# A chunkwise recurrence on one core: decay applied to the queries, and 64-row halves for the products beside it

## The reference

```
m_t = max(b + m, max_s(log_D));  inter_w = exp(b + m - m_t)
s   = (q k^T) * exp(log_D - m_t)
num = s v + inter_w * (q C);     den = sum(s) + inter_w * (q n)
h   = num / max(|den|, exp(-m_t))
C   = decay * C + (ws * k)^T v;  n likewise
```

## Time and profile before

| | |
|---|---|
| median of 3 runs | 1169.8 us (1169.3 to 1170.23) |
| the profiled execution, first to last instruction (span) | 1168.5 us |
| median of the runs less that span | 1.3 us |
| TensorE busy | 1158.7 us, 99% |
| weight loads (PEld) busy | 946.1 us, 81% |
| VectorE, GpSimd, ScalarE busy | 678.5, 455.9, 359.2 us |
| granted TensorE clock, mean | 0.999 of full speed |
| front of head 0 (calls and scores) | 486.6 to 498.9 us |
| recurrence, heads 0 to 3 | 498.9 to 677.2 us |

### The profile page before, as it was taken

How to read it: one execution, slowest core, us unless ns; L and a number is a source line. 1 busy time by engine, 2 the same in 40 slices (tenths; PEclk the granted TensorE clock), 3 DMA queues, 4 the chain that set the end, 5 groups by cost and what they waited for, 6 DMA issues and landing times.

```text
span 1168.5 us, 17252 instructions
## 1 busy us (share of the span) xinstructions
PE 1158.7 (99%) x6599; PEld 946.1 (81%) x6599; DVE 678.5 (58%) x1249; ACT 359.2 (31%) x720; POOL 455.9 (39%) x437
## 2 busy tenths in 40 slices
PE   9999999999999999999999999999999999999997
PEld 6888888888888868888878888878988887777786
DVE  5645557334368502157777883894699434556668
ACT  6312121100012212445665631242111134553322
POOL 2424222223333223354657656304223323455534
PEclk9999999999999999999999999999999999999999
DMA  7321121343312112300113242123121130133113
GB/s 241 109 81 45 36 81 36 123 152 114 109 36 72 64 64 90 101 23 23 50 34 112 88 171 73 72 100 95 40 88 36 37 100 1 38 122 124 39 38 141
DMA packets 75075, 93.56 MB, mean 80 GB/s; under 512 B 13938, under 2 KB 54090, under 8 KB 74483
## 3 DMA queue, kind: packets, MB, share of 16 engines
q1 hardware_dynamic: 67270, 88.73, 22.7%
q10 hardware_dynamic: 7724, 3.74, 1.2%
HBM read 75.11 MB, written 18.92 MB: 80 GB/s over the span
## 4 chain that ended last, share of the span: by engine, by line
PE 93%; DVE 4%; DMA 1%; ACT 1%; issue 1%; POOL 0%; ACTq 0%; DVEq 0%; POOLq 0%
PE bank L918 22%; PE bank L920 22%; PE bank L919 22%; PE bank L1219 4%; PE bank L1194 4%; PE wide L1210 2%; PE wide L1412 2%; PE bank L1158 1%; PE bank L1147 1%; PE bank L1135 1%; PE wide L920 1%; PE wide L919 1%; PE wide L918 1%; PE bank L1387 1%; DVE h L1910 1%; PE wide L1387 1%
## 5 line engine op out<-in xcount | busy, mean ns | idle before, releaser
L687 POOL CAST whi<-wraw 128x2048 fp32r<-128x2048 f32 x31 | 58.8, 1898 | 454.1 <-PE bank L920 404.1
L918 PE MATMUL bank<-u_hi,wlo 128*128 128x512 f32 x488 | 190.4, 390 | 0.0
L920 PE MATMUL bank<-u_hi,whi 128*128 128x512 f32 x488 | 189.9, 389 | 0.0
L919 PE MATMUL bank<-u_lo,whi 128*128 128x512 f32 x488 | 189.9, 389 | 0.0
L689 POOL TENSOR_TENSOR wlo<-wraw,whi 128x2048 fp32r<-128x2048 f32 x32 | 153.1, 4784 | 3.0 <-ACT whi L2488 0.5
L918 PE MATMUL bank<-x_hi,wlo 128*128 128x512 f32 x312 | 123.5, 396 | 0.0
L920 PE MATMUL bank<-x_hi,whi 128*128 128x512 f32 x312 | 121.6, 390 | 0.0
L919 PE MATMUL bank<-x_lo,whi 128*128 128x512 f32 x312 | 121.5, 389 | 0.0
L918 PEld LDWEIGHTS bank<-u_hi,wlo 128*128 128x128 f32 x488 | 91.6, 188 | 19.9 <-POOL wlo L689 0.8
L920 PEld LDWEIGHTS bank<-u_hi,whi 128*128 128x128 f32 x488 | 91.6, 188 | 19.0
L919 PEld LDWEIGHTS bank<-u_lo,whi 128*128 128x128 f32 x488 | 91.6, 188 | 18.9
(11 more groups left out here) (391 smaller groups left out, 2440.9 us busy)
## 6 DMA issues: line engine op xcount, KB each, us to landing
wraw<-in_w_in SPq DMA_DIRECT2D x26, 1024.0 KB, 5.5
wraw<-in_w_out SPq DMA_DIRECT2D x12, 1024.0 KB, 5.1
xr<-in_x SPq DMA_DIRECT2D x8, 512.0 KB, 7.3
hst<-in_x SPq DMA_DIRECT2D x4, 1024.0 KB, 5.0
hpool<-hst SPq DMA_DIRECT2D x4, 1024.0 KB, 4.1
smz<-mzs SPq DMA_DIRECT2D x16, 256.0 KB, 2.0
h<-hpool SPq DMA_DIRECT2D x4, 1024.0 KB, 7.5
resid<-h SPq DMA_DIRECT2D x8, 512.0 KB, 2.6
```

The costliest lines, as they stand in the source:

```text
L687: g_.tensor_copy(whi[w % 2][:, :, :], wraw[:, :, :]).then_inc(s["w_hi"], 1)
L918: pe.matmul(ps, al, bh, start=(k == 0), stop=False)
L919: pe.matmul(ps, ah, bl, start=False, stop=False)
L920: return pe.matmul(ps, ah, bh, start=False, stop=(k == nk - 1))
```

## The change

The decay of the positions moves from the inter product's result to the queries, and the inter product then adds up in the same bank as Pm times v. The rows of decay (`r4[:, 0, :]`) are stored beside the stabilisers in DRAM and spread with them, so a spread moves 256 KB instead of 128. GpSimd multiplies the queries of unit n+2 by the spread row (`scale_q`) in its turn for unit n, into four buffers `qsi`, `qsj`. ScalarE's scaled copy and VectorE's `total` go.

The calls of `headwise` for keys and values become half as many and twice as long: eight blocks, each in two halves of 64 rows, the halves into two neighbouring banks. Queries in units 0 to 3, keys in 4 and 6, values in 8 and 10; none in 5, 7, 9 and 11. `turn_h` of heads 0 to 2 is made of halves too, in banks 0 and 1. The queries' calls and scores alternate between banks 0 and 1. ScalarE empties a keys' call with one instruction of 1024 elements, a values' call with two of 512.

```diff
-    nm_t = nc.dram_tensor("nmax", [ROWS, P], F32)
+    nm_t = nc.dram_tensor("nmax", [ROWS, 2, P], F32)
...
-        FILL = {m: (m,) for m in range(12)}
+        FILL = {0: 0, 1: 1, 2: 2, 3: 3, 4: 4, 6: 5, 8: 6, 10: 7}
...
 # SyncE
-                    sp_.dma_start(nm_t.ap(), nM[:, :]).then_inc(s["o_rel"], 16)
-                    sp_.wait_ge(s["o_rel"], 32)
+                    sp_.dma_start(nm_t.ap()[:, 0, :], nM[:, :]).then_inc(s["o_rel"], 16)
+                    sp_.wait_ge(s["a_r"], 3)
+                    sp_.dma_start(nm_t.ap()[:, 1, :], r4[:, 0, :]).then_inc(s["o_rel"], 16)
+                    sp_.wait_ge(s["o_rel"], 48)
...
 # GpSimd
+            def scale_q(n):
+                h, p, d, ck, _ = unit(n)
+                i = upd_of(h, p - 1, d)
+                if d == 0:
+                    g_.wait_ge(s[f"l_br{n // 2 % 4}"], 16 * (n // 8 + 1))
+                if i >= 4:
+                    g_.wait_ge(s["t_inter"], i - 3)
+                g_.tensor_tensor(scaled_q(i), qTs[h % 2][:, :, ck * P:(ck + 1) * P],
+                                 carried(n // 2, d).unsqueeze(1).to_broadcast([P, 2, P]), ALU.mult
+                                 ).then_inc(s["g_qs"], 1)
...
                     if n % 2 == 0 and n < 62:
                         masked(n // 2 + 1)
+                    if n % 16 < 14:
+                        scale_q(n + 2)
                     if n in GATE_MUL:
                         gate_mul(GATE_MUL[n])
...
 # TensorE
-            turns, free = [0], [1, 5, 2, 6, 3, 7]
+            turns, free = [0], [5, 6, 7, 4]
...
+                both(m2, "a_hq", 10 * h + (i + 1 if i < 6 else 2 * i - 4))
+                if i == 6:
+                    pe.wait_ge(s["g_bdh"], 2 * h + 2)
+                for block in range(8):
+                    t, m = i % 2 * 4 + block // 2, block % 2
+                    tt = slice(t * P, (t + 1) * P)
+                    for half in range(2):
+                        rows = slice(64 * half, 64 * half + 64)
+                        out_ = bank[2 * m2 + half][:, block * 64:(block + 1) * 64]
+                        if i < 6:
+                            mm = pe.transpose(out_, cc[rows, 2 * h + m, tt],
+                                              cst[rows, C_ID + 64 * half:C_ID + 64 * half + 64])
                         else:
-                            mm = pe.matmul(ps[:, b * P:(b + 1) * P], um[:, 2 * h + m, tt], bdh[:, m, :],
-                                           start=True, stop=True)
+                            mm = pe.matmul(out_, um[rows, 2 * h + m, tt], bdh[rows, m, rows], start=True, stop=True)
...
+                    sums = take(4 + n % 4, "v_h", n + 1)
                     if p:
                         i = upd_of(h, p - 1, d)
+                        pe.wait_ge(s["g_qs"], i + 1)
                         pe.wait_ge(s["v_C"], 2 * i + 2)
-                        ps = take(0, "a_tmp", i + 1)
                         for k in range(2):
-                            mm = pe.matmul(ps[:, 0:AUG], q[:, k, ck * P:(ck + 1) * P], Cst[:, d, k, :],
-                                           start=(k == 0), stop=(k == 1))
+                            mm = pe.matmul(sums[:, 0:AUG], scaled_q(i)[:, k, :], Cst[:, d, k, :],
+                                           start=(k == 0), stop=False)
...
                     pe.wait_ge(s["g_P"], n + 1)
-                    ps = take(4 + n % 4, "v_h", n + 1)
-                    pe.matmul(ps[:, 0:AUG], Pm[:, n % 2, :], v[:, ck, :], start=True, stop=True
+                    pe.matmul(sums[:, 0:AUG], Pm[:, n % 2, :], v[:, ck, :], start=(p == 0), stop=True
                               ).then_inc(s["t_intra"], 1)
...
 # VectorE
-                    total(h, n)
                     if p or h in (0, NH - 1):
                         state(h, n)
-                    total(h, n + 1)
-                    if p:
-                        ve.wait_ge(s["v_tot"], upd_of(h, p - 1, 1) + 1)
+                    ve.wait_ge(s["t_intra"], n + 2)
...
 # ScalarE
-                    if p:
-                        i = upd_of(h, p - 1, d)
-                        ps = filled(ac, "t_inter", i + 1, "a_tmp", i + 1)
-                        if n >= 4:
-                            ac.wait_ge(s["v_h"], n - 3)
-                        ac.activation(tmps[p % 2][:, d, :], ps[:, 0:AUG], ACT.Copy, scale=cols[:, 0, r:r + 1]
-                                      ).then_inc(s["a_tmp"], 1)
```

More of the change, by code:

```diff
@@ L238, in build @@
          cva, mzs, _m, wgx, gx, gr, ga, wkx, kx, ak,
-         hc0, yt0, kwb, Amat, hc1, Cst, tmpi, Pm, bdh, gs, nM, cols,
+         hc0, yt0, kwb, Amat, hc1, Cst, qsi, Pm, bdh, gs, nM, cols,
          rif, rl, rb, r4, rz, rp, rpc, rms8, rn,
@@ L307, in build @@
         rcx = sb("rcx", [P, 2, 2])
-        bank = [ctx.enter_context(nc.psum_tensor(f"bank{i}", [P, 512], F32)) for i in range(4)]
+        duo = [ctx.enter_context(nc.psum_tensor(f"bank{m}", [P, S], F32)) for m in range(2)]
         wide = [ctx.enter_context(nc.psum_tensor(f"wide{m}", [P, S], F32)) for m in range(2)]
-        bank += [wide[i // 2][:, i % 2 * 512:(i % 2 + 1) * 512] for i in range(4)]
+        duo += wide
+        bank = [duo[i // 2][:, i % 2 * 512:(i % 2 + 1) * 512] for i in range(8)]
         names = (
@@ L1124, in fill, with both, headwise @@
                 return take(free[turns[0] % len(free)], name, value)
-            def headwise(h, i):
-                n, i = i // 4, i % 4
-                if n == 0:
+            def both(m, name, value):
+                take(2 * m, name, value)
+                return take(2 * m + 1, name, value)
+            def headwise(h, i, m2=0):
+                if i < 4:
                     m, nh = i // 2, i % 2
@@ L1167, in turn_h @@
                 if h < NH - 1:
-                    ps = fill("a_t1", n + 1)
-                else:
-                    ps = ring_x("v_y1", 12 + 2 * i + 1)
+                    both(0, "a_t1", n + 1)
+                    for b in range(4):
+                        for half in range(2):
+                            rows = slice(64 * half, 64 * half + 64)
+                            mm = pe.transpose(bank[half][:, b * 64:(b + 1) * 64],
+                                              hcs[h % 2][rows, 4 * nh + b, mt * P:(mt + 1) * P],
+                                              cst[rows, C_ID + 64 * half:C_ID + 64 * half + 64])
+                    mm.then_inc(s["t_h"], 1)
+                    return
+                ps = ring_x("v_y1", 12 + 2 * i + 1)
                 for b in range(4):
@@ L1223, in units @@
                         turn_h(h - 1, TURN[n % 16])
-            for i in range(12):
-                headwise(0, i)
+            for i in range(8):
+                headwise(0, i, i % 4)
+            free[:] = [0, 1]
             for b in range(2):
                 scores(0, b)
-            del free[1:]
             for h in range(NH):
@@ L2341, in evac_features @@
                                   ).then_inc(s["a_hq"], 1)
[L2342 to L2345, removed]
+                    return
+                ac.wait_ge(s["t_hw"], 8 * h + i + 1)
+                t = slice(i % 2 * 4, i % 2 * 4 + 4)
+                if i < 6:
+                    ac.activation(kts[h % 2][:, t, :].rearrange("p t (m u c) -> p u (t m) c", m=2, c=64),
+                                  duo[m2][:, :].rearrange("p (u b c) -> p u b c", u=2, c=64), ACT.Copy
+                                  ).then_inc(s["a_hq"], 1)
+                    return
+                for half in range(2):
+                    ac.activation(vs[h % 2][:, t, 0:HD].rearrange("p t (m u c) -> p u t m c", m=2, c=64)[:, half],
+                                  bank[2 * m2 + half][:, :].rearrange("p (t m c) -> p t m c", t=4, c=64), ACT.Copy
+                                  ).then_inc(s["a_hq"], 1)
             def evac_scores(h, b):
@@ L2434, in units @@
                         turned_h(4 * (h - 1) + TURN[m])
-            for i in range(8):
-                evac_features(0, i)
+            for i in range(6):
+                evac_features(0, i, i % 4)
             ac.wait_ge(s["v_cols"], 1)
             weight(0)
-            for i in range(8, 12):
-                evac_features(0, i)
+            for i in range(6, 8):
+                evac_features(0, i, i % 4)
             for b in range(2):
```

88 lines of the change are left out of this document (41 added, 47 removed).

## The result

The change takes 1172.8 us (median of 5 runs, 1172.53 to 1175.31) against 1169.74 for the kernel before on the same chip: ratio 1.0031, 95% interval 1.0019 to 1.0042. The forecast was 1166.1 us and "faster"; both were wrong. The profiled execution's span is 1171.0 us against 1168.5.

The account below looks back on a forecast made before the run. The prediction took TensorE, busy 99% of the span, to bound the kernel. Its terms summed to −3.7 us, taking the profiled span from 1168.5 to 1164.8 and the median to 1166.1 us, range 1162.5 to 1172.

Parts of the forecast that it names:

- keys in halves, six calls: Six key calls beside the recurrence: sixteen half transposes cost 0.83 us against 0.87 for eight full ones, −0.2 us.
- turns in halves: Turns on TensorE's path in heads 1, 2 and first in 3: eight halves 0.58 us against 0.44, +1.3 us.
- values in halves, six calls: Six value calls beside the recurrence: 1.33 us each in halves against 1.79 full, −2.7 us (−3.3 to +2.0).
- front of head 0: Before head 0, two key and two value calls in a row share one switch: −1.9 us.
- stalls after the table loads: Third unit of heads 1 to 3: waits behind ScalarE's table loads, tmp and Cst come back in full, −1.7 us.
- turned bank: Behind turns: TensorE's waits for the bank ScalarE is still emptying come back, −1.8 us.
- units 33 and 49: Second unit of heads 2 and 3: scaling on GpSimd makes Pm late, +0.65 and +0.25, together +0.9 us.
- end of head 3: Last eight units, no filler left: five scalings on GpSimd delay Pm, +2.4 us, bounds 0 and 3.5.
- no overlap: Upper bound for a value call in halves, 16 × 64 × 1.76 ns + 0.33 = 2.13 us.
- rival 2: Value halves don't overlap, 2.13 us each instead of 1.33, also before head 0: +6.4, 1172.5 us; chance 0.1.
- rival 3: TensorE's stalls stay because another wait ends last in their place: +3.5, 1169.6 us, no difference; chance 0.2.
- rival 1: GpSimd becomes the bound in all heads, if a scaling costs about 0.98 us, not 0.73: 1174 us; chance 0.15.

Follow-up runs that it names:

- full products for the values: The changed kernel with the values' calls as eight full products of 128 rows in two banks, all else kept: 1170.8 us.
- unscaled queries: The changed kernel without any scaling of the queries, the decay left out of the inter product: 1168.33 us.
- keys on ScalarE: The changed kernel with head 3's weighted keys made by ScalarE instead of GpSimd, query scaling staying on GpSimd: 1169.75 us.
- narrow moving data: The changed kernel with 32 instead of 64 moving columns in each values' half product, weights unchanged: 1173.93 us in one run.

## Why the prediction was wrong, point by point

| term | predicted, us | measured, us | shown by |
|---|---|---|---|
| keys in halves, six calls | −0.2 | −0.2 | starts at 601.17 |
| turns in halves | +1.3 | +1.2 (8 of them; the others lie in head 3's end) | starts at 658.27 |
| values in halves, six calls | −2.7 | +2.0 | full products for the values |
| front of head 0 | −1.9 | −0.4 | starts at 486.23, 494.47 |
| stalls after the table loads | −1.7 | −1.75 | starts at 601 |
| turned bank | −1.8 | −1.55 | starts behind turns |
| units 33 and 49 | +0.9 | +1.15 | unscaled queries |
| end of head 3 | +2.4 | +2.6 | unscaled queries, keys on ScalarE |
| sum | −3.7 | +3.1 (the windows: +3.2) | |

The step that failed is "Values": "I take 32 records at 0.031 = 1.0", and the same rate for 96 records in front of head 0. These two terms are off by 4.7 and 1.5 us, 6.2 of the 6.9 us between the forecast's sum and that of the windows. The 0.031 came from transposes and was carried over to fp32 products. I had checked it against the score products of 64 rows and 32 output rows, which load only 32 weight columns and stream 288: a form in which the load can't be the bound, so it said nothing about this one. What is true of the earlier trace rows is that row halves overlap; here they overlap too (starts 1 ns apart), but a full product does the work of two halves in the same two passes. Sixteen pairs of half passes take 1.84 us (half of the 3.67 in front of head 0), as do sixteen full ones (half of 3.68 at the same place with full products), and the mode switch comes on top. The bound "no overlap", 2.13, was met to the digit by another mechanism.

So rival 2, chance 0.1, met the time by luck: 1172.5 forecast for it, 1172.8 measured. Its reason, that the halves don't overlap, is refuted by their starts and by narrow moving data: one behind the other, half the stream would have shortened the call. The Trainium skill (TensorE: Matmul & The Clock Gate, section LDWEIGHTS) has a load last its columns over 1.2 GHz, however few rows. For the values the trace agrees: 0.11 us for a pair of passes with 128 weight columns, 0.06 with 64 (there with half the output rows as well). The prediction set this rule aside because transposed halves take 0.062, which they still do, so the sentence "it doesn't bear that out" was true of transposes and was applied to the wrong kind of product. By the page's rule the call would have been 2.04 and the kernel about 1171.7 us; the measured call is 2.13.

The other steps held. The stalls named did go, with their sizes, once the decay was moved; rival 3 (another wait takes their place) is refuted by the kernel with only the decay moved, where none of them is left. Of the turned bank's waits, 2.0 us when all starts behind turns are compared, 0.11 stayed at each of four score calls (1.00 and 1.86 us where 0.97 and 1.78 are free), so 1.55 came back. GpSimd was priced rightly at the end of head 3 (+2.4, got +2.6) and a little low at units 33 (+0.7 with its neighbours) and 49 (+0.45, its update in unit 48 followed by 1.26 us instead of 0.86). In unit 33 the query call is followed by 1.49 us instead of 0.86, as Pm stands behind scaling and gating. The timeline there, all engines, kernel after:

```profile
590.99 1.26 POOL L787 TENSOR_TENSOR yt<-yt,smzb 128x512 f32<-128x512 f32 x1
591.23 1.02 PE L1166 MATMUL bank<-cc,Amat 128*128 128x512 f32 x2
...
592.21 0.46 POOL L808 TENSOR_TENSOR Pm<-ST,Wb 128x128 f32<-128x128 f32 x1
```

Pm starts 592.21 and had started 591.79 before, in a head that now begins 0.3 us earlier: the 0.70 us of one scaling.

One figure of the working is off without effect: the prediction's own costs add up to 44.9 us for TensorE in head 2, not "some 44.6", which moves rival 1's threshold for a scaling only a little.

The range of 1162.5 to 1172.0 missed the result by 0.8 us: its upper edge left rival 2 outside, though its working stood at 1172.5 with a bound of the values' row behind it.

## What to carry to other kernels

Before a rate is carried from one product to another, ask what sets it in the form where it was seen (stream, weight load, or a single pass against two), and take it only from a form with the same weight columns, the same passes and a stream as short. Splitting rows in halves pays where each half runs in less than a full pass, as the transposes do, and long rows of them share one switch (about 0.1 us on either side); a full fp32 product of 128 weight and 128 moving columns, split in two, gained nothing here. When work moves to an engine with room on average, price it in the stretch that has no filler left (here the last eight units), and move something else off that engine there in the same edit.

## What the runs showed of the hardware that was not expected

- Two row halves of an fp32 product with 128 weight columns and 64 moving columns take 0.11 us a pass together, as a full pass does (0.89 us for 8). With 32 moving columns nothing changes; with 64 weight columns it is 0.06. The transposed halves have the same form in the trace, 64 by 128 with 64 columns, and take 0.062 in a single pass, their loads 138 ns instead of 188. Why a transpose's load is the faster one no run here shows.
- VectorE and GpSimd slowed each other down where a VectorE operation with two operands in SBUF ran beside GpSimd. In the kernel after this is more frequent: VectorE's mix of the turned head (L1798) took 733 to 1552 ns, 994 in the mean of 11, against 785 in the mean of 12 before, and six of 64 Pm took 0.84 to 0.92 us, about twice the usual 0.45; before, none took over 0.47. Without any scaling (the unscaled kernel) the mix took 814 ns in the mean of 12, but six Pm were as long. So the scaling accounts for most of the longer mixes and not for the long Pm. The timeline of the kernel after:

```profile
571.33 1.28 POOL L795 TENSOR_TENSOR ym_lo<-yt,ym_hi 128x512 fp32r<-128x512 f32 x1
571.61 1.54 DVE L1798 SCALAR_TENSOR_TENSOR yt<-cc,VT,yt 128x512 f32<-128x512 f32 x1
...
572.55 0.91 POOL L808 TENSOR_TENSOR Pm<-ST,Wb 128x128 f32<-128x128 f32 x1
```

  VectorE ends only after GpSimd's 1.28 us, and the Pm that starts at 572.55 ends 0.3 us behind VectorE instead of after 0.46. The Trainium skill (SBUF — State Buffer, section SBUF: two separate sides) says that the two share a pair of ports that one instruction holds alone, also when a VectorE operation has two SBUF inputs; these rows and the 2.09 us pair of scalings on VectorE agree that each waits for the other. They don't show that the one that waits stands still: VectorE is done 0.54 us after GpSimd, less than the 0.73 of its shortest such operation. It is at least a part of why moving the scaling to VectorE, where it took 0.69 us in the mean (0.41 at the least) in place of 0.73, saved nothing.
- The granted clock of TensorE fell to its lower level for 3.4 us although the engine was never idle: behind 64 half products of 32 moving columns in a row, not behind the same 64 with 64 columns. It was seen in one execution.
